# PEER gates placed by accumulating scatters of single cells instead of one-hot matmuls

## What is computed

```python
s_top, i_top = lax.top_k(scores, 16)          # per token, head and key half: 16 of 128
cand = s_top[:, :, 0, :, None] + s_top[:, :, 1, None, :]
best, pos = lax.top_k(cand, 16)               # per token and head: 16 of 256 pairs
expert_idx = take_along_axis(i_top[0] * 128 + i_top[1], pos)
gates = softmax(best)
# per token, over its 8 heads x 16 picks:
act = gelu(h . expert_u[expert_idx])
out = sum(act * gates * expert_v[expert_idx])
x = LayerNorm(ALPHA * x + out)
```

## Time and profile before

| | us |
|---|---|
| median of 3 executions | 2012.72 |
| lowest and highest | 2007.53, 2030.52 |
| the profiled execution, its own time | 2017.35 |
| its span in the profile | 2015.6 |
| TensorE busy | 1963.3 (97%) |
| VectorE busy | 1106.5 (55%) |
| GpSimd busy | 889.4 (44%) |
| ScalarE busy | 680.6 (34%) |

### The profile page before, as it was taken

One profiled execution on the slowest core, in us unless ns is written; L12 is line 12 of the kernel. 1 busy time (PEld: TensorE's weight loads), 2 busy tenths in 40 slices (PEclk: granted clock), 3 DMA queues, 4 the chain that ended last, 5 costly groups with the idle time before them and its releaser, 6 DMA issues.

```text
span 2015.6 us, 24624 instructions
## 1 busy us (share of the span) xinstructions
PE 1963.3 (97%) x9433; PEld 1563.4 (78%) x9433; DVE 1106.5 (55%) x2263; ACT 680.6 (34%) x1029; POOL 889.4 (44%) x502
## 2 busy tenths in 40 slices
PE   7999999999989999999999999999998999999998
PEld 5766655888778888888888888888886778878876
DVE  4022212311330599883688888500076879888887
ACT  4623323323222333233333333332332333333332
POOL 6313111344344144545333333344487857576540
PEclk9999999999999999999999999999999999999999
DMA  5202110232422144444465566654488989999993
GB/s 192 75 31 74 53 48 21 73 110 95 167 84 94 61 148 142 141 150 147 161 196 178 182 194 198 209 198 147 141 318 301 374 332 384 337 351 381 352 354 115
DMA packets 164774, 368.39 MB, mean 183 GB/s; under 512 B 15265, under 2 KB 80929, under 8 KB 164530
## 3 DMA queue, kind: packets, MB, share of 16 engines
q1 hardware_dynamic: 51264, 184.57, 26.1%
q10 hardware_dynamic: 90866, 115.06, 16.8%
q0 software_dynamic: 22528, 67.19, 8.9%
HBM read 305.96 MB, written 60.82 MB: 182 GB/s over the span
## 4 chain that ended last, share of the span: by engine, by line
PE 74%; DMA 11%; DVE 8%; issue 3%; POOL 3%; ACT 1%; SPq 0%; ACTq 0%; DVEq 0%; POOLq 0%
PE bank L432 22%; PE bank L434 21%; PE bank L433 21%; DMA act<-activation_scratch 11%; PE bank L715 3%; DVE w_lo L1334 2%; DVE bank L1199 2%; POOL weight L395 2%; PE bank L564 1%; DVE act L1323 1%; DVE wt_lo L1327 1%; PE bank L586 1%; PE bank L603 1%; PE bank L611 1%; PE bank L682 1%
## 5 line engine op out<-in xcount | busy, mean ns | idle before, releaser
L383 POOL TENSOR_TENSOR w_lo<-stage,w_hi 128x1024 fp32r<-128x1024 f32 x224 | 543.1, 2433 | 910.3 <-ACT w_hi L773 910.3
L432 PE MATMUL bank<-x_hi,w_lo 128*128 128x512 f32 x1376 | 543.6, 395 | 7.6 <-DVE x_lo L1056 5.0
L434 PE MATMUL bank<-x_hi,w_hi 128*128 128x512 f32 x1376 | 537.4, 391 | 0.0
L433 PE MATMUL bank<-x_lo,w_hi 128*128 128x512 f32 x1376 | 536.9, 390 | 0.0
L773 ACT ACTIVATE w_hi<-stage 128x1024 fp32r<-128x1024 f32 x348 | 358.9, 1041 | 21.9 <-PE bank L434 8.9
L432 PE MATMUL bank<-w_hi,wt_lo 128*128 128x512 f32 x768 | 301.7, 393 | 21.0 <-DVE wt_lo L1327 21.0
L432 PEld LDWEIGHTS bank<-x_hi,w_lo 128*128 128x128 f32 x1376 | 259.1, 188 | 62.5 <-DVE x_lo L1056 5.9
L434 PEld LDWEIGHTS bank<-x_hi,w_hi 128*128 128x128 f32 x1376 | 259.1, 188 | 55.3
L434 PE MATMUL bank<-w_hi,wt_hi 128*128 128x512 f32 x768 | 300.4, 391 | 0.0
L433 PE MATMUL bank<-w_lo,wt_hi 128*128 128x512 f32 x768 | 300.4, 391 | 0.0
L433 PEld LDWEIGHTS bank<-x_lo,w_hi 128*128 128x128 f32 x1376 | 259.4, 189 | 52.4
(11 more groups left out here) (217 smaller groups left out, 1902.4 us busy)
## 6 DMA issues: line engine op xcount, KB each, us to landing
stage<-in_expert_uT SPq DMA_DIRECT2D x128, 512.0 KB, 3.5
stage<-in_expert_v SPq DMA_DIRECT2D x128, 512.0 KB, 7.2
stage<-in_mix_stream SPq DMA_DIRECT2D x84, 512.0 KB, 3.5
gates<-gate_scratch ACTq DMA_DIRECT2D x32, 768.0 KB, 6.2
act<-activation_scratch ACTq DMA_DIRECT2D x32, 768.0 KB, 12.7
activation_scratch<-act_out_a ACTq DMA_DIRECT2D x64, 256.0 KB, 2.3
activation_scratch<-act_out_b ACTq DMA_DIRECT2D x64, 256.0 KB, 2.3
gate_scratch<-gstage_a ACTq DMA_DIRECT2D x6, 2048.0 KB, 11.1
```

The costliest lines, as they stand in the source:

```text
L383: nc.gpsimd.tensor_tensor(w_lo[:, slot, 0:width], stage[:, slot % STAGE, 0:width], w_hi[:, slot, 0:width], ALU.subtract).then_inc(split_do ...
L432: mm(dst, l_lo, r_hi, start=first, stop=False)
L433: mm(dst, l_hi, r_lo, start=False, stop=False)
L434: return mm(dst, l_hi, r_hi, start=False, stop=last)
```

## The change

The one-hot tables, their matmuls, copies and DRAM writes are gone, and so are the transposes. In their place:

- `gate_scratch` becomes a plain [i, j, token] array. SP fills it with zeros in 32 DMAs of 768 KB from a 128x128 tile of zeros, one behind each of the loads of tiles 10 to 41.
- VectorE computes for each block and pick the number of the cell (`cells`), next to the finished gate. GpSimd adds each gate to its cell in DRAM by an indirect DMA that accumulates: 3 blocks x 128 picks = 384 of them, 128 cells of 4 bytes each (`scatter_head`). A head's 16 go out together; the next head of the same block waits until they have landed, since it may hit the same cell. Heads of two blocks alternate where they can.
- The dense tokens are now 0 to 383. The last block is gathered, not the first.
- GpSimd makes only the low parts of U tiles 0 to 13. VectorE makes all others, of U and V. A counter of estimated time (`passed`) decides when the kernel is built where among the top-16 steps each of these subtractions stands.
- ScalarE loads the activations of units 0 and 1 at tile 120 and their gates at tile 126, after waiting for all scatters. Later units load activations first, then gates, the latter in rows of 1536 bytes (6144 before). The first weight is rounded after tile 127.

```diff
-GB = 32
-GT = 4
+DENSE = TB - 1
+HEAD_PICKS = TOPK
+FILLS = 32
+FIRST_FILL = 10
+TILE_US = 5.44
+POOL_TILES = 14
+FIRST_BEST_US = -13.0
+EXP_AT = {7: 0, 21: 1, 36: 2, 51: 3}
-EXP_AT = {9: 0, 20: 1, 32: 2, 44: 3}
-TURN_AT = {27: 1, 39: 2, 50: 3}
-FIRST_GATE = 50
-GATE_SPAN = 48
...
 def on_vector(tile):
-    return tile >= NKEY + 4
+    return tile >= POOL_TILES
...
-    gate_dram = nc.dram_tensor("gate_scratch", [NUNIT, P, NGB, UNIT * GB], F32, kind="Internal").ap()
+    gate_dram = nc.dram_tensor("gate_scratch", [NKEY, P, ND], F32, kind="Internal").ap()
...
+            def zero_fill(f):
+                if f == 0:
+                    sp.wait_ge(zeros_made, 1)
+                u = NKEY * ND // P // FILLS
+                cells = gate_dram.rearrange("i j t -> (i j t)").rearrange("(p n c) -> p n c", p=P, c=P)
+                sp.dma_start(cells[:, u * f:u * f + u, :],
+                             zeros[:].unsqueeze(1).broadcast_to([P, u, P])).then_inc(zero_filled, 16)
...
-            for tile in range(NKEY + 4):
+            for tile in range(POOL_TILES):
                 split_low(first_expert + tile, (first_expert + tile) % RING, QW)
+            gate_cells = gate_dram.rearrange("i j (t o) -> (i j t) o", o=1)
+            def scatter_head(b, h):
+                if h == 0:
+                    pool.wait_ge(scat_ready, 2 * b + 2)
+                else:
+                    pool.wait_ge(scattered[b], 16 * HEAD_PICKS * h)
+                for k in range(h * HEAD_PICKS, (h + 1) * HEAD_PICKS):
+                    nc.gpsimd.indirect_dma_start(out=gate_cells,
+                                                 out_offset=bass.IndirectOffsetOnAxis(ap=scat_idx[:, b, k:k + 1], axis=0),
+                                                 in_=scat_gate[:, b, k:k + 1], in_offset=None,
+                                                 compute_op=ALU.add).then_inc(scattered[b], 16)
+            pool.wait_ge(zero_filled, 16 * FILLS)
+            for h in range(4):
+                scatter_head(0, h)
+            for b in range(DENSE):
+                for h in range(4):
+                    scatter_head(b, h + 4)
+                    if b + 1 < DENSE:
+                        scatter_head(b + 1, h)
...
             for tile in range(NKEY):
-                if tile in TURN_AT:
-                    turn_picks(TURN_AT[tile])
                 score_tile(tile)
-                for g in range(groups_by(tile - 1), groups_by(tile)):
-                    gate_group(g)
...
+            def load_gates(u):
+                if u == 0:
+                    for b in range(DENSE):
+                        sc.wait_ge(scattered[b], 16 * NPICK)
+                sc.dma_start(gates[:, u % 2], gate_dram[UNIT * u:UNIT * u + UNIT].rearrange("c p t -> p c t")
+                             ).then_inc(gates_in[u % 2], 16)
...
                 store_tile(t)
-                for g in range(groups_by(t - 1), groups_by(t)):
-                    evac_group(g)
-                if t == last_group_tile + 2:
-                    for half in range(2):
-                        sc.wait_ge(gm_written[half], 16 * NGB // 2)
-                    load_unit(0)
-                    load_unit(1)
+                if t == NKEY - 8:
+                    load_acts(0)
+                    load_acts(1)
                 if t == NKEY - 2:
-                    round_weight(0)
+                    load_gates(0)
+                    load_gates(1)
+            round_weight(0)
...
+            clock, next_split = [FIRST_BEST_US], [POOL_TILES]
+            def passed(us):
+                clock[0] += us
+                while next_split[0] <= clock[0] / TILE_US + 3:
+                    split_value(next_split[0])
+                    next_split[0] += 1
+                    clock[0] += 1.25
```

More of the change, by code:

```diff
@@ L59 @@
 TAIL_TILES = 4
-def groups_by(tile):
-    return max(0, min(NGROUP, (tile - FIRST_GATE + 1) * NGROUP // GATE_SPAN))
 def picks_by(v):
@@ L185, in build @@
         aidx = at("aidx", [P, NPICK], U32, E + 10)
+        zeros = at("zeros", [P, P], F32, E + 13)
         spare = at("spare", [P, P], F32, E + 10.5)
@@ L237, in build @@
         sc_done, sc_evac = sem("sc_done"), sem("sc_evac")
-        best_ready, gate_exp, picks_ready, picks_turned = sem("best_ready"), sem("gate_exp"), sem("picks_ready"), sem("picks_turned")
-        picks_evac, parts_ready, eidx_ready = sem("picks_evac"), sem("parts_ready"), sem("eidx_ready")
+        best_ready, gate_exp, eidx_ready = sem("best_ready"), sem("gate_exp"), sem("eidx_ready")
+        zeros_made, zero_filled, scat_ready = sem("zeros_made"), sem("zero_filled"), sem("scat_ready")
+        scattered = [sem(f"scattered{b}") for b in range(DENSE)]
         gathered = [sem(f"gathered{i}") for i in range(GATHER)]
@@ L1207, in weigh_picks, with split_value @@
                 step(v.tensor_tensor(weight[:, r], weight[:, r], g0[:, r], ALU.mult))
+            clock, next_split = [FIRST_BEST_US], [POOL_TILES]
+            def split_value(tile):
+                n = first_expert + tile
+                dve.wait_ge(hi_done, n + 1)
+                v.tensor_tensor(w_lo[:, n % RING, :], stage[:, n % STAGE, :], w_hi[:, n % RING, :],
+                                ALU.subtract).then_inc(value_split, 1)
+            def passed(us):
[4 more added lines that the diff above has]
+                    clock[0] += 1.25
             def top16(vals, idx, src, rows_n):
+                us = 0.2 * rows_n if rows_n == HP else 0.34 * rows_n
                 for a in range(rows_n):
@@ L1212, in top16 @@
                 step(ins)
+                passed(us)
                 for a in range(rows_n):
@@ L1284, in _, with cells @@
-            for t in range(1, TB):
+                dst = g0 if t == DENSE else scat_gate[:, t, :]
+                ins = v.tensor_tensor(dst.rearrange("p (h k) -> p h k", h=PH), gx, share, ALU.mult)
+                if t < DENSE:
+                    ins.then_inc(scat_ready, 1)
+                else:
+                    step(ins)
+            def cells(dst, t, width):
+                step(v.tensor_scalar(spare[:], spare[:], float(width), float(t * P), ALU.mult, ALU.add))
+                step(v.tensor_scalar(spare[:], spare[:], token[:], None, ALU.add))
+                return v.tensor_copy(dst, spare[:])
@@ L1285, in _, with expert_numbers @@
+            def expert_numbers(t):
+                step(v.scalar_tensor_tensor(out=spare[:], in0=ijg[:, t % 2, 0, :], scalar=float(NKEY), in1=ijg[:, t % 2, 1, :],
+                                            op0=ALU.mult, op1=ALU.add))
+            for t in range(TB):
                 first_level(t)
-                finish_gates(t - 1)
                 second_level(t)
-                if t >= 2:
-                    split_gates(t - 1)
                 decode(t)
-            finish_gates(TB - 1)
@@ L1312, in _ @@
-            for g in range(NGROUP):
-                if g == 8:
-                    split_gates(TB - 1)
-                one_hots(g)
+                expert_numbers(t)
+                if t < DENSE:
+                    cells(scat_idx[:, t, :], t, ND).then_inc(scat_ready, 1)
+                else:
+                    v.tensor_copy(eidx[:], spare[:])
+                    cells(aidx[:], t, S).then_inc(eidx_ready, 1)
+                finish_gates(t)
+                passed(3.0)
+            for tile in range(next_split[0], NKEY):
+                split_value(tile)
@@ L1321, in weigh @@
                     dve.wait_ge(act_in[u % 2], 16 * (u // 2 + 1))
-                a = act[:, u % 2, k, :].rearrange("p (b t) -> p b t", b=NGB)
-                v.tensor_tensor(a, a, gates[:, u % 2, :, k, :], ALU.mult).then_inc(wt_mul, 1)
+                a = act[:, u % 2, k, :]
+                v.tensor_tensor(a, a, gates[:, u % 2, k, :], ALU.mult).then_inc(wt_mul, 1)
             def weight_low(w):
@@ L1328, in weight_low @@
                                 ALU.subtract).then_inc(wt_done, 1)
-            def split_value(tile):
-                n = first_expert + tile
-                dve.wait_ge(hi_done, n + 1)
-                v.tensor_tensor(w_lo[:, n % RING, :], stage[:, n % STAGE, :], w_hi[:, n % RING, :],
-                                ALU.subtract).then_inc(value_split, 1)
             for tile in range(NKEY, NKEY + 3):
```

126 lines of the change are left out of this document (26 added, 100 removed).

## The result

The changed kernel is slower: median **2091.88 us** (2088.69 to 2094.07, four executions) against 2019.51 us of the kernel before on the same chip, ratio 1.034, 95% interval 1.029 to 1.038. Forecast was 1940; the range reached to 2125.

The account below looks back on a forecast made before the run. TensorE, busy for 97% of the span, was taken as the bound. From 2017.35 us, -72.9 for U, +3.9 for V's start and -4 for the gathers gave 1944.3, as a median 1940 us; range 1928 to 2125.

Parts of the forecast that it names:

- Issue time goes by the count of offsets there: GpSimd in U: an accumulating scatter issues like a gather with 128 offsets, 0.95 us, 1.45 us with gaps and VectorE.
- Rival 1: GpSimd's scatters: an accumulating one takes longer to issue, or lands late, so V starts late and time is lost; chance 0.33.
- with half as much again: GpSimd: scatter issue of 1.42 us, scatters end at 1532, V from 1544, median 2096 us.
- The point from which the sign turns: GpSimd: from a scatter issue time of about 1.20 us on, scatters end at 1445 and the gain is used up.
- The margin: End of U: scatters done at 1345, 35 us before ScalarE asks for the gates, 0.09 us per scatter.
- TensorE's saving: U stage: gate-group matmuls and three transposes go, GELUs stay 5.44 us apart, U takes 696.3 us; -72.9 us.
- The start of V: Between U and V: gates asked for at 1379.9, TensorE starts V at 1387.9, +3.9 us after U's end (2 to 8).
- The zeros: SP's queue from tile 10: 32 fills of 768 KB add 25 MB to lightly used DMA engines; 0, at worst 3 us.
- VectorE in U: Low parts and picks: VectorE waits now and then for ScalarE, picks ready at 734, 815, 897, 980; 0, if lagging 10 to 30.
- The last scatter: GpSimd: start at 746, plus 557 for 384 scatters, 27 for waits and an allowance of 15, gives 1345 us.
- 0.75 for each subtraction: GpSimd in U: each VectorE subtraction, one per 5.44 us, delays the scatters by 0.75 us, hence 1.45 us per scatter.
- The allowance of 15 for the picks: GpSimd until 990 us: VectorE's picks add more two-input work that slows scatters; 15 us.

Follow-up runs that it names:

- experiment 1: Changed kernel with all 384 scatters writing plainly instead of accumulating, waits kept: 1940.77 us, ratio 0.969 to the kernel before.
- experiment 2: Changed kernel without the third block's 128 scatters and ScalarE's wait for them: 1945.28 us, ratio 0.970 to the kernel before.
- experiment 7: Changed kernel with VectorE summing gates of equal picks, plain scatters writing running sums, exponentials moved, same result: 1944.25 us, ratio 0.968 to the kernel before.
- experiment 5: Changed kernel with VectorE's subtractions for U cut from 1024 to 8 columns: timed at 2078.98 us against the changed kernel's 2091.73.
- first kernel of experiment 4: Changed kernel with fewer cells per scatter: block 0 adds 64, block 1 writes 64 plainly, block 2 adds 96: 1984.38 us, one execution.
- second kernel of experiment 4: Changed kernel with fewer cells per scatter: block 0 adds 16, block 1 writes 16 plainly, block 2 adds 112: 2195.83 us.
- experiment 6: The changed kernel again, unedited, run twice: 2085.34 us, and 2091.73 us, the latter 1.037 of the kernel before.

## Why the prediction was wrong, step by step

**The step that failed** is "Issue time goes by the count of offsets there, so I take 0.95 us here". The gathers' median was right for scatters as such (0.959, experiment 1) and wrong for one that accumulates: 1.547, that is 1.63 times the gathers' 0.946. Rival 1 came true, in its form "with half as much again": it said a V start at 1544 and 2096 us; measured 1516.3 and 2091.88 (the time is so near only because V, longer by 18 us, made up for most of the earlier start). The other way to the same end that it names, additions that land over 25 us after their issue, is out: they land in 2.9 to 5.5 us (experiment 2). The point from which the sign turns was given as an issue of about 1.20 us; the measured value is well beyond, and both kernels whose scatters stay below it (experiments 1 and 7) are faster than the one before. I gave the case 0.33 because "against it stands only that both gathers cost alike". That was weak ground: two gathers that differ in bytes say something on bytes, and nothing on an added operation. The margin was 0.09 us for each of 384 instructions, on a price that no row showed; a forecast that needs such a price to be exact should not have had 0.50.

The Trainium skill (Collectives: The Full Stack, section Stop ④ — SDMA + CCE: where bytes move and the add happens) counts two reads and a write for an add. Read as a rule for the issue, as the prediction did, that would have been twice the price, and 2274 us. The measured 1.63 times, and a surcharge of which three quarters (0.433 of 0.588 us) are there with 16 cells already, speak against reading it that way. Of the DMA engines' own time more below.

**What held.**
- TensorE's saving: GELUs are 5.44 apart up to the last tile (1374.88, 1380.32), U takes 1385.6 - 689.1 = 696.5 us against 696.3 forecast. Without the hole the whole comes to 1940.77 against 1940. That this is so exact is partly luck: the sum's last terms are smaller than what V's length varies by, and V before was 549.8 us long in its profile (1456.9 to 2006.7), not the "some 543" that matmuls and waits added up to.
- The start of V: 2.7 us of gap in experiment 1, forecast 3.9. The gathers start 1.9 us ahead of V there (1384.24), forecast 4.
- The zeros: the stretch 100:340 has 111 GB/s, forecast 43 + 105, as the fills reach over 32 to 346 us. Fills land in 5.5 to 9.1 us. No cost of them is seen: TensorE's U begins at 689.1 here, but at 686.8 and 684.0 in experiments 1 and 7, which have the same fills, against 687.7 before.
- VectorE in U: it waits 337.0 us in 98 times for ScalarE's high parts, and TensorE never for it. Picks are ready at 734.6, 819.1 and 900.7 (forecast 734, 815, 897); nine heads wait, 19.1 us in all where I had 27.
- The last scatter, had there been no addition: forecast 1345, measured 1305.5 (its issue began at 1304.1). Two terms were too high: 0.75 for each subtraction (0.39), and the waits (17.4 for 27). The allowance of 15 for the picks was about right: all 384 took 424.2 us, 56 more than 384 medians; the 103 subtractions that fell among them explain 40 at 0.39, which leaves 16.

**VectorE against GpSimd.** The pair of rows showed an overlap that cost 0.8 us, and I made it the rule for every subtraction. Over a whole stretch it is 0.12 us for adding scatters and 0.39 for others. The Trainium skill (SBUF — State Buffer, section Who interferes with whom) says that such two-input operations don't hold up descriptor writing; experiment 5 finds an effect, of 13.5 us over all scatters, so the sentence isn't exact. For adding scatters (0.12) it was nearer than my 0.75, for plain ones (0.39) about as far off. One pair of rows can't be told from a coincidence; a mean over a stretch can.

**The account of the profiled execution**, against experiment 1 (1940.28 in its own profiled execution): V starts 130.2 us later, V is 18.2 longer, together 2088.7, measured 2088.69.

## What to carry to other kernels

Price an unseen form of an instruction as unknown, and compute first from which price on the sign of the result turns; if the nearest row lies within a fifth of that point, forecast by the chance of crossing it and not by the row. A scatter that accumulates costs more to issue than one that writes (1.547 and 0.959 us here), mostly per instruction and little per element, so sum on an idle engine and write plainly. An engine that works ahead of a join costs nothing until its end passes the join, and then every microsecond of it: what counts is the last start against the time of the request.

## What was not expected of the hardware

**Additions load the DMA engines.** In the stretch 1000:1250 the kernel after and the one without additions move the same 146 GB/s, with shares of 0.67 and 0.43, and GpSimd issues fewer of the adding ones (132 against 179). The stretch without additions:

```profile
1000.00:1250.00 250.00, 250.00 (x1105) 207.08 (x1104) 56.20 (x46) 71.14 (x92) 188.22 (x179) 1.00 0.43 146
```

So the share of 0.24 is the additions', of four bytes each; plain single cells don't show in it (the kernel before has 0.42 in 747:990). In U there was room for it. An adding scatter also lands later, in 2.9 to 5.5 us (median 3.5, experiment 2), a plain one in 2.1 to 4.3 (2.4).

With the share goes a count of packets. GpSimd's DMA queue (packets, MB, share of 16 engines) in the kernel before, which has the gathers alone on it, in the one of experiment 1, and in the changed kernel:

```profile
q0 software_dynamic: 22528, 67.19, 8.9%
q0 software_dynamic: 34816, 67.41, 9.7%
q0 software_dynamic: 77824, 67.41, 17.0%
```

With the gathers' 22528 taken off, a plain scatter is 32 packets and an adding one 144, for the same 128 cells. Both kernels of experiment 4 (51200 and 47104 packets) fit a rule of one packet for each cell and 16 more for a scatter that adds, and 32 for a plain one whatever its cells. The issue price doesn't follow this count: by that rule either kind has 32 packets with 16 cells, and yet they take 1.280 and 0.847 us.

**A stretch at the lower clock that nothing in the program asks for.** In three of the six profiles of kernels with a hole of over 100 us, beginning some 35 to 75 us after V has started, TensorE runs for 40 to 50 us at or near a granted clock of 0.50, the lower of its levels (1.2 of 2.4 GHz), with gaps between matmuls that wait for nothing in the profile. From the changed kernel as timed in experiment 6, 40 us of it and the 40 behind:

```profile
1560.00:1600.00 40.00, 18.25 (x42) 10.46 (x43) 8.43 (x12) 4.99 (x8) 22.74 (x25) 0.55 0.48 140
1600.00:1640.00 40.00, 40.00 (x178) 33.14 (x177) 35.49 (x55) 14.09 (x19) 26.96 (x22) 1.00 0.99 364
```

V takes 561.6, 568.3 and 559.3 us in the three profiles with it, and 559.9, 550.4 and 545.6 in the three without. The first kernel of experiment 4, with a hole of 33 us, takes 554.5 and has none. None of the four profiles of kernels without a hole (before, and experiments 1, 2 and 7) has one so long, though short dips stand there too (0.73 over 1537:1547 before, 0.66 over 1486:1496 in experiment 1). But the second kernel of experiment 4, with its scatters over at 1372 and no hole, has one of 240 us in the middle of U, in its only execution. The stretch 900:1100 of that kernel:

```profile
900.00:1100.00 200.00, 55.31 (x131) 33.15 (x130) 26.83 (x128) 7.35 (x10) 154.81 (x146) 0.55 0.13 20
```

So it can't be put down to the hole alone, and what causes it stays open, as do the 2 to 25 us that V is longer. They don't bear on the verdict: the hole of 131 us does. The clock is at 0.52 in the hole too, and in the profile after the first eight matmuls of V stand 0.43 to 0.56 us apart instead of 0.23, which is under 2 us.
